# Earlier scores and loads in pieces, scans and high/low parts spread over chunks, sums 128 columns wide, in a fused three-layer block kernel

## The reference

```
first_block:  xn = rmsnorm(x);  q, k, v, xr, gr, ga, gb = split(xn @ w_in)
              ya = banded_attention(q, k, v, rel_bias) @ w_attn_out       (16 heads of 64)
              xc = causal_conv4(xr);  r, i = sigmoid(block matmuls of xc)
              a = exp(-8 r softplus(-lambda));  h = scan(a, sqrt(1-a^2) * i * xc)
              yb = (h * gelu(gr)) @ w_rnn_out
              x += (sigmoid(ga) * ya + sigmoid(gb) * yb) @ w_o
              x += (silu(g) * up) @ w_ffn_out;   x = rmsnorm(x)
second_block: x += gated_deltanet(rmsnorm(x)): q, k, v = silu(conv4(.)), unit-norm q and k,
              decay g and beta from 16 columns, chunks of 128 tokens solved as a triangular
              system, output norm per head, gate silu(z), @ w_out
              x += relu(rmsnorm(x) @ w_up)^2 @ w_down
              x += moba_attention(rmsnorm(x)) @ w_out;  x += mlp;  rmsnorm
```

## Time and profile before

| | |
|---|---|
| median of 3 runs | 1193.99 us (1193.93 to 1196.65) |
| the profiled execution | 1196.81 us |
| its span, first to last instruction | 1195.1 us |
| PE busy | 1144.0 us (96%) |
| DVE busy | 752.3 us (63%) |
| ACT busy | 564.9 us (47%) |
| POOL busy | 219.7 us (18%) |
| mean granted clock of PE | 0.984 |
| read from HBM | 185.29 MB |

### The profile page before, as it was taken

One profiled execution on the slowest core, in us unless ns is written; L12 is line 12 of the kernel. 1 busy time (PEld: TensorE's weight loads), 2 busy tenths in 40 slices (PEclk: granted clock), 3 DMA queues, 4 the chain that ended last, 5 costly groups with the idle time before them and its releaser, 6 DMA issues.

```text
span 1195.1 us, 21847 instructions
## 1 busy us (share of the span) xinstructions
PE 1144.0 (96%) x8900; PEld 1106.9 (93%) x8900; DVE 752.3 (63%) x913; ACT 564.9 (47%) x721; POOL 219.7 (18%) x226
## 2 busy tenths in 40 slices
PE   4999899999999999998999999999989999999997
PEld 4999789999999999998999998889989999888996
DVE  3745975576566543589968567763366757776433
ACT  4546456535454343456635355543344445554331
POOL 4895001502000000246373020000030002000001
PEclk9999999999999999899899999999999999999999
DMA  9654443655555555345420056555535445565541
GB/s 259 225 175 142 141 141 108 199 167 164 176 196 190 177 177 179 103 140 177 137 76 2 9 176 199 181 177 186 188 118 191 163 139 178 179 197 187 175 140 36
DMA packets 154852, 187.34 MB, mean 157 GB/s; under 512 B 6400, under 2 KB 143776, under 8 KB 154784
## 3 DMA queue, kind: packets, MB, share of 16 engines
q1 hardware_dynamic: 149072, 183.51, 47.3%
q10 hardware_dynamic: 5712, 2.86, 0.9%
HBM read 185.29 MB, written 1.07 MB: 156 GB/s over the span
## 4 chain that ended last, share of the span: by engine, by line
PE 86%; DVE 9%; issue 2%; ACT 2%; DMA 1%; POOL 0%; SPq 0%; DVEq 0%; POOLq 0%; ACTq 0%
PE PS L332 20%; PE PS L333 19%; PE PS L334 19%; PE PS L388 10%; PE PS L390 5%; DVE WL L328 2%; DVE XHL L485 1%; PE PS L397 1%; PE PS L396 1%; PE PS L395 1%; ACT WH L319 1%; PE PS L1798 1%; DMA RAW<-in_w_in 1%; PE PS L1784 1%; PE PS L677 1%
## 5 line engine op out<-in xcount | busy, mean ns | idle before, releaser
L328 DVE TENSOR_TENSOR WL<-RAW,WH 128x2048 fp32r<-128x2048 f32 x173 | 409.2, 2366 | 251.8 <-ACT WH L319 251.8
L319 ACT ACTIVATE WH<-RAW 128x2048 fp32r<-128x2048 f32 x173 | 330.0, 1909 | 251.3 <-PE PS L334 203.1
L332 PE MATMUL PS<-XHL,WH 128*128 128x256 f32 x1184 | 346.9, 293 | 27.3 <-DVE WL L328 18.8
L333 PE MATMUL PS<-XHL,WH 128*128 128x256 f32 x1184 | 340.5, 288 | 0.0
L334 PE MATMUL PS<-XHL,WL 128*128 128x256 f32 x1184 | 340.2, 287 | 0.0
L332 PEld LDWEIGHTS PS<-XHL,WH 128*128 128x128 f32 x1184 | 233.2, 197 | 33.1 <-DVE WL L328 18.4
L333 PEld LDWEIGHTS PS<-XHL,WH 128*128 128x128 f32 x1184 | 233.2, 197 | 0.3
L334 PEld LDWEIGHTS PS<-XHL,WL 128*128 128x128 f32 x1184 | 232.7, 197 | 0.0
L332 PE MATMUL PS<-HH,WH 128*128 (+1 forms) x688 | 195.0, 283 | 4.3 <-DVE SG L1581 2.8
L333 PE MATMUL PS<-HL,WH 128*128 (+1 forms) x688 | 194.7, 283 | 0.0
L334 PE MATMUL PS<-HH,WL 128*128 (+1 forms) x688 | 194.7, 283 | 0.0
(11 more groups left out here) (287 smaller groups left out, 1538.3 us busy)
## 6 DMA issues: line engine op xcount, KB each, us to landing
RAW<-in_mlp_w_up SPq DMA_DIRECT2D x32, 1024.0 KB, 5.5
RAW<-in_mlp_w_down SPq DMA_DIRECT2D x32, 1024.0 KB, 4.9
RAW<-in_w_in SPq DMA_DIRECT2D x28, 1024.0 KB, 5.2
RAW<-in_w_ffn_in_pairs SPq DMA_DIRECT2D x22, 1024.0 KB, 5.1
RAW<-in_dn_w_in SPq DMA_DIRECT2D x16, 1024.0 KB, 5.7
RAW<-in_mb_w_in SPq DMA_DIRECT2D x12, 1024.0 KB, 5.2
RAW<-in_w_ffn_out SPq DMA_DIRECT2D x11, 1024.0 KB, 5.0
RAW<-in_w_attn_out SPq DMA_DIRECT2D x4, 1024.0 KB, 5.1
```

The source lines that it names most:

```text
L319: act.activation(WH[:, k], RAW[:, k], ACT.Copy).then_inc(hi_done, 1)
L328: dve.tensor_tensor(WL[:, k], RAW[:, k], WH[:, k].bitcast(F32), ALU.subtract).then_inc(lo_done, 1)
L332: pe.matmul(out, wh, xh, start=start, stop=False, skip_group_check=True)
L333: pe.matmul(out, wh, xl, start=False, stop=False, skip_group_check=True)
```

## The change

- The x parts and chunks 0 and 1 are loaded in quarters: x part, quarter of chunk 0, and so on, then chunk 1's quarters. ACT and DVE split by quarters, PE multiplies chunks 0 and 1 by quarters (`multiply_pieces`), each with a wait of its own.
- The gate weights and the table rows are loaded from SP's queue, between chunks 2 and 3; the decay inputs' rows and the bias from ACT's queue in qk chunk 2. An exp on one column stands first on ACT.
- The first norm: DVE adds the squares instead of POOL, the sums are behind chunk 1 and the rows in the middle of chunk 2 (SUMS_AT 3, ROWS_AT 4). ACT takes the root after the split of chunk 3, DVE the reciprocal after the low half of chunk 3; chunk 0 is read out after that. POOL's preparation of W2, G23 and WBA goes behind the convolution.
- The softplus starts at the head of DVE's list and ends in qk chunk 0; ACT waits for it before the first gate pair (`sp_ready`).
- The roots go from v chunk 1 to v chunk 2. The scans go two blocks each into attention steps 0 to 3.
- The first scores wait for the read-out of the last qk chunk.
- The high and low parts of the gated scan go one by one into the ao chunks, after a wait for the last gab chunk's matmul.
- All sums over partitions with 1, 2 or 16 columns stream 128 columns: ONES whole, W2 and WBA repeated. The results wanted are the first columns. The output norm's columns are in another order.

```diff
@@ names
+        piece_in = [sem(f"piece_in{p}") for p in range(6)]
+        def piece_of(c, p):
+            return (slice(None), c, slice(512 * p, 512 * p + 512))
+        def piece_landed(c, p):
+            return piece_in[3 * c + p] if p < 3 else raw_in[c]
+        def fetch_piece(eng, c, p):
+            dst = RAW[piece_of(c, p)].rearrange("p (k n) -> p k n", k=2)
+            eng.dma_start(dst, source("xr", c)[:, 2 * p:2 * p + 2, :]).then_inc(piece_landed(c, p), 16)
+        def split_hi_piece(act, c, p):
+            act.wait_ge(piece_landed(c, p), 16)
+            act.activation(WH[piece_of(c, p)], RAW[piece_of(c, p)], ACT.Copy).then_inc(s_.hi_piece if p < 3 else hi_done, 1)
+        def multiply_pieces(pe, st):
+            c = st.base
...
+            for p in range(4):
+                if c == 0:
+                    pe.wait_ge(s_.xl_ready, p + 1)
+                if p < 3:
+                    pe.wait_ge(s_.lo_piece, 3 * c + p + 1)
+                else:
+                    pe.wait_ge(lo_done, c + 1)
+                for b in range(2):
+                    part = slice(b * P, b * P + P)
+                    for k in (2 * p, 2 * p + 1):
+                        mm = product(pe, PS[:, c, b * TOK:(b + 1) * TOK], h[:, k, part], l[:, k, part], XH[:, k], XL[:, k],
+                                     k == 0 and b == 0, k == KB - 1)
+            mm.then_inc(mm_done, 1)
-        SUMS_AT = [2, 2, 1, 2, 2, 2]
-        ROWS_AT = [3, 3, 2, 5, 3, 5]
+        SUMS_AT = [3, 2, 1, 2, 2, 2]
+        ROWS_AT = [4, 3, 2, 5, 3, 5]
@@ norm_sums
-                        mm = pe.matmul(PS[:, 4, 2 * c:2 * c + 2], XN[:, j, c * P:(c + 1) * P], W2[:, j],
-                                       start=(j == 0), stop=(j == KB - 1))
+                        mm = pe.matmul(PS[:, 4, 2 * c:2 * c + P].rearrange("p (r e) -> p r e", e=2), XN[:, j, c * P:(c + 1) * P],
+                                       W2[:, j, None, :].to_broadcast([P, P // 2, 2]), start=(j == 0), stop=(j == KB - 1))
...
-                    mm = pe.matmul(PS[:, sums_bank(m), c:c + 1], XN[:, 0, c * P:(c + 1) * P], ONES[:, 0:1], start=True, stop=True)
+                    mm = pe.matmul(PS[:, sums_bank(m), c:c + P], XN[:, 0, c * P:(c + 1) * P], ONES[:], start=True, stop=True)
@@ sync
-            for name, n in SEGMENTS:
-                steps(sp, seg[name], lambda st: fetch(sp, st), head=SLOTS if name == "xr" else 0)
+                fetch_piece(sp, 0, p)
+            for p in range(4):
+                fetch_piece(sp, 1, p)
+            fetch(sp, Step(seg["xr"], 2, None))
+            sp.wait_ge(s_.ext_ready, 1)
+            sp.dma_start(ext_dram, EXT[:]).then_inc(s_.ext_out, 16)
+            sp.wait_ge(s_.wri_zero, 1)
+            sp.wait_ge(s_.pool, 2)
...
+            fetch(sp, Step(seg["xr"], 3, None))
+            for name, n in SEGMENTS[1:]:
+                steps(sp, seg[name], lambda st: fetch(sp, st))
@@ scalar
+            act.wait_ge(s_.const, 1)
+            act.activation(SUM[:, 0:1], EPSC[:], ACT.Exp)
             act.wait_ge(s_.vec_in, 16)
             for p in range(4):
                 norm_high(act, 0, p, squares=False)
+                split_hi_piece(act, 0, p)
+            squares(act, 0, 0)
+            squares(act, 0, 1)
+            act.wait_ge(s_.ey_done, 1)
+            act.activation(SMALL[:, 1, 0:8], SMALL[:, 1, 0:8], ACT.Exp, scale=-1.0).then_inc(s_.sm_ready, 1)
+            for p in range(4):
+                split_hi_piece(act, 1, p)
+            squares(act, 0, 2)
+            squares(act, 0, 3)
...
             for st in (Step(seg["xr"], j, None) for j in range(4)):
                 split_hi(act, st)
-                if st.j == 0:
-                    act.wait_ge(s_.const, 1)
+                if st.j == 1:
                     norm_root(act, 0)
...
             for st in (Step(seg["qk"], j, None) for j in range(8)):
                 split_hi(act, st)
+                if st.j == 2:
+                    late_inputs()
+                if st.j == 0:
+                    act.wait_ge(s_.sp_ready, 1)
                 gate_pair(st.j)
...
-                if st.j == 1:
+                if st.j == 2:
                     root(0)
                     root(1)
...
             for st in (Step(seg["ao"], j, None) for j in range(4)):
+                p = st.j
                 split_hi(act, st)
-            for p in range(4):
+                act.wait_ge(mm_done, seg["ao"].first)
                 act.wait_ge(s_.hs_ready, p + 1)
                 act.activation(XH[:, 2 * p:2 * p + 2], XN[:, 2 * p:2 * p + 2], ACT.Copy).then_inc(s_.yh_done, 1)
@@ vector
             for p in range(4):
                 norm_low(dve, 0, p)
+                split_lo_piece(dve, 0, p)
+            for p in range(4):
+                split_lo_piece(dve, 1, p)
+            dve.wait_ge(s_.sq_done, 4)
+            ch(dve.tensor_tensor(XN[:, 0:4], XN[:, 0:4], XN[:, 4:8], ALU.add))
...
             for st in (Step(seg["xr"], j, None) for j in range(4)):
                 split_lo(dve, st)
                 if st.j == 0:
+                    continue
+                if st.j == 1:
                     norm_scale(dve, ch, 0)
                     dve.wait_ge(s_.wri_zero, 1)
+                    read_out(Step(seg["xr"], 0, None), XR[:, 0:2, 3:TOK + 3])
                 read_out(st, XR[:, 2 * st.j:2 * st.j + 2, 3:TOK + 3])
...
-                if st.j == 3:
-                    scan(0)
...
-                if n == 1:
-                    scan(1)
+                if n < 4:
+                    scan(n)
...
                 split_lo(dve, st)
+                dve.wait_ge(s_.yh_done, j + 1)
+                dve.tensor_tensor(XL[:, blk], XN[:, blk], XH[:, blk].bitcast(F32), ALU.subtract).then_inc(s_.y_done, 1)
                 dve.wait_ge(mm_done, st.count())
@@ tensor
-                if st.j == 1:
+                if st.j < 2:
+                    multiply_pieces(pe, st)
                     pe.wait_ge(s_.const, 2)
-                times_x(0)(st)
+                    norm_point(pe, 0, 2 * st.j + 1)
+                else:
+                    times_x(0)(st)
...
-            c = seg["gr"].first - 1
+            c = seg["v"].first - 1
             pe.wait_ge(freed[c % SLOTS], c // SLOTS + 1)
             pe.wait_ge(s_.gates_done, 16)
             attn_scores(pe, 0)
...
-                            mm = pe.matmul(PS[:, 3, 256 + 16 * c:272 + 16 * c], H[:, k, c * P:(c + 1) * P], WBA[:, k],
+                            mm = pe.matmul(PS[:, 3, 256 + 16 * c:384 + 16 * c].rearrange("p (r e) -> p r e", e=16),
+                                           H[:, k, c * P:(c + 1) * P], WBA[:, k, None, :].to_broadcast([P, KB, 16]),
...
-                        mm = pe.matmul(PS[:, 4 + u, n:n + 1], sq, ONES[:, 0:1], start=True, stop=True)
+                        mm = pe.matmul(PS[:, 4 + u, n:n + P], sq, ONES[:], start=True, stop=True)
...
-                        mm = pe.matmul(PS[:, 4, 8 * c + h:8 * c + h + 1], OSQ[:, h, c * P:(c + 1) * P], ONES[:, 0:1], start=True, stop=True)
+                        mm = pe.matmul(PS[:, 4, 2 * h + c:2 * h + c + P], OSQ[:, h, c * P:(c + 1) * P], ONES[:], start=True, stop=True)
```

More of the change, by code:

```diff
@@ L260, in build @@
           amf_out yf_out ty_out zg_done vn0 vn0_out s_done s_out w_done w_out vn1 vn1_out o_done o_out osq osum osd
-          orows gated uq_zero yy oo low_out""".split()
+          orows gated uq_zero yy oo low_out hi_piece lo_piece sp_ready""".split()
         s = {n: sem(n) for n in names}
@@ L753, in _ @@
                 sp.dma_start(H[:, 2 * p:2 * p + 2], a["x"].rearrange("(j p) t -> p j t", p=P)[:, 2 * p:2 * p + 2]).then_inc(x_in[p], 16)
-            for name, n in SEGMENTS:
-                steps(sp, seg[name], lambda st: fetch(sp, st), head=SLOTS if name == "xr" else 0)
+                fetch_piece(sp, 0, p)
[6 more added lines that the diff above has]
+            sp.wait_ge(s_.pool, 2)
+            for r, w in enumerate(("w_rg_r", "w_rg_i")):
+                for e in range(2):
+                    sp.dma_start(WRI[64 * e:64 * e + 64, r, :, 64 * e:64 * e + 64],
+                                 a[w].rearrange("(j e) d f -> e d j f", e=2)[e]).then_inc(s_.wri_in, 16)
+            fetch(sp, Step(seg["xr"], 3, None))
+            for name, n in SEGMENTS[1:]:
+                steps(sp, seg[name], lambda st: fetch(sp, st))
             for p in range(4):
@@ L809, in _ @@
                         pool.wait_ge(s_.conv_done, j + 1)
+            pool.wait_ge(s_.row_in, 48)
+            fg, g3 = vec_at["final_norm_g"], vec_at["mix_norm_g_2"]
+            pc(pool.memset(W2[:, :, 0:1], 1.0))
+            pc(pool.tensor_tensor(W2[:, :, 1], VEC[:, fg:fg + KB], VEC[:, fg:fg + KB], ALU.mult))
+            pc(pool.tensor_tensor(G23[:], VEC[:, fg:fg + KB], VEC[:, g3:g3 + KB], ALU.mult))
+            pc.wait(pool)
+            pool.tensor_tensor(WBA[:], WBA[:], G23[:, :, None].to_broadcast([P, KB, 16]), ALU.mult).then_inc(s_.prep, 1)
+            pool.wait_ge(s_.prep, 1)
```

(39 more changed lines are left out.)

51 lines of the change are left out of this document (17 added, 34 removed).

## The result

The changed kernel takes 1174.29 us (median, 1173.04 to 1178.35) against 1193.96 (1193.92 to 1196.65) for the kernel before beside it: 0.9836 of it, 95% interval 0.9807 to 0.9864, 19.7 us less. A second series gave 1174.04 against 1194.40: 0.9824 (0.9807 to 0.9842). The forecast was 1171.2, range 1165 to 1180.

What follows compares the result with a forecast made beforehand. TensorE bounds the kernel (86% of the span), so gains come where it waits or runs at half clock: terms of 24.0 less 1.2 charges give 22.8 off 1196.8, less 2.8 for the median: 1171.2 us, range 1165 to 1180.

Steps and rivals of the forecast that it cites:

- the charges of 1.2: Taken off the summed gain: 0.5 for the convolution on POOL and 0.7 for one possible clock fall.
- The charge of 0.7: New short idle stretches before 524 and 679 us may drop the clock: one fall at even odds, 1.7 us.
- Head: Start of the kernel up to the query chunks: PE starts near 7 us, query chunks at 36.3 instead of 45.3, minus 9.0.
- Rival B's first half: Head: pieces move at 227 GB/s (2.7 us); all of B, loads late, head minus 4, 1176 us, 12%.
- Attention: Start of attention: PE's 3.84 us wait and the clock fall after it go, DVE ready 0.7 late; minus 4.8.
- another low half: Start of attention, DVE: second low half before the shift, after one at up to 3.87; minus 4 if POOL slows it too.
- rival C: Start of attention: scores early, but DVE with POOL beside it reaches the shift as late as before; 4.8 back, 1176, 8%.
- Attention output to recurrent output: PE's 1.5 us wait goes as the gated scan's parts move to the attention-output chunks; minus 1.5.
- Norm and decay inputs: Second layer: wide sums keep the clock up, 4.4 for PE, but DVE and ACT then set the pace; minus 2.9.
- Unit norms: Wide sums keep full clock: sums 4.8 to 3.6, chunks 7.7 and 7.2 to 5.75; minus 4.7.
- Output norm: 16 transposes go from 3.40 to 1.75 us at full clock, DVE's products then bind; minus 1.1.
- Rival D: Query chunks: POOL's convolution becomes the bound and the kernel slower; at 11 us a block the time is 1199; 2%.

Runs made afterwards that it cites:

- a_rc: The changed kernel with the first norm's root ahead of chunk 3's split on ACT and the reciprocal ahead of chunk 3's low half on DVE: 1171.84 us.
- a_whole: The changed kernel with chunks 0 and 1 loaded in one load of 1 MB each, splits and products still by quarters: 1175.10 us, ratio 0.9838.
- a_rows: The changed kernel with the three loads for the decay inputs' rows back at the head of ACT's queue, bias still late: 1178.80 us, ratio 0.9862.
- a_shift: The changed kernel with DVE's first attention shift ahead of the second gate chunk's low half, and first scaling ahead of the next low half: 1170.84 us, ratio 0.9798.
- b_sums: The kernel before with only the sums changed, every sum over partitions 128 columns wide: 1187.67 us, ratio 0.9936.
- a_again: The changed kernel run again, unedited, beside the three single parts: 1174.04 us.
- a_root1: The changed kernel with only the roots back in the second v chunk: 1178.04 us.

## Why the prediction came out as it did

**The time.** The forecast was 3.1 below the median. The sum made against the profiled execution (22.8; 23.5 was measured) came close, 1174.0 against 1173.36, in part by luck: attention gave 2.7 less than its term, the head 1.2 and the other parts 1.0 more, and the charges of 1.2 were not used. What put the median off is the frame. I took 2.8 off because the profiled run of before was that much above its median; but the profiled run of after was 0.9 below its own, and the medians differ by only 19.7 and 20.4. What the traces show to differ between runs of the same kernel is when loads land and which idle stretches drop the clock, and a profile shows one draw of that. The places where PE idles, and in how many of the traces the clock fell behind them:

| idle stretch of PE | us | fell |
|---|---|---|
| first scores (kernels with the old wait) | 3.8 | 3 of 3 |
| decay's transposes, 550 | 3.2 | 9 of 14 |
| reciprocal in chunk 2 | 1.9 to 3.7 | 4 of 7 |
| read-out of chunk 0 (a_rc) | 2.1 | 0 of 1 |
| output chunks, 656 (wide sums) | 2.0 | 5 of 10 |
| first transposes of attention | 1.9 to 2.7 | 6 of 8 |
| 30 us into the second block, 508 (wide sums) | 1.7 | 0 of 10 |
| feed-forward's second product | 1.5 | 0 of 14 |

A fall of 3.4 us costs 1.4 to 1.5 at attention and at the output chunks, and nothing at 550, where traces with and without it reach the unit norms' rows equally soon; one of 6.8 there costs 0.9 to 1.1. The charge of 0.7 for one such fall was of the right kind; the wait before the output chunks, at five in ten, is the place.

**Head** (9.0 forecast, 10.2 here, 7.1 to 10.5 over the six traces of this head). The first matmul at 6.9 to 7.4 was right, the wait for the reciprocal too (2.3 against 1.8). The clock rose 4.3 us after the first matmul here (2.9 to 6.2 over the traces) against 7.5 in the sum; but that was not the term that counted. The term is chunk 3's arrival, forecast 23 and measured 21.9, from which the rest follows at the forecast's durations. One step was wrong in kind: I took the early 227 GB/s as the rate at which x lands and the later 341 for the rest, and costed the move of the decay inputs' rows at nothing. Those rows were the cause: putting them back takes the rate to 240 and costs 4.8 us of the median, over half of the head's gain of 8.4. Rival B's first half (pieces are slow) falls with a_whole. The size rule of the Trainium skill that stood behind it, on the page "DMA: Bandwidth & Descriptors", is measured there on loads that GpSimd issues; for SP's loads of 256 KB beside those of 1 MB it doesn't show here. The same page of the Trainium skill has under Specifications a least transfer of 512 bytes for full rate; the packets of a_rows agree with that, and I had not weighed it.

**Attention** (4.8 forecast, 2.1 here). The scores started 0.2 us behind the start of the last V matmul and the old wait went, as forecast; the next late thing was DVE, as forecast, but at 1.9 us instead of 0.7. The step that failed is "another low half" at 2.3 us: POOL's products stretched both low halves, had only one in their reach, and moving the roots by a chunk put them beside two. I had priced that case at 0.8 us; it cost 1.2 of wait, and with it came the fall of the clock that the sum had counted as gone (1.7 forecast, 1.5 measured). It is rival C's mechanism at part strength. a_shift shows it: with one low half out of POOL's way the gain is 4.6. The two POOL products take 2.8 and 4.4 us, and each low half ends about a plain low half's time after a product has ended (107.2 and 111.6). The Trainium skill, "SBUF — State Buffer", section "Who interferes with whom", has it that a DVE instruction with two inputs in SBUF and a GpSimd instruction that reads SBUF lock each other out; low half and root product are such a pair, and the rows agree with blocking rather than sharing.

**Attention output to recurrent output** (1.5): 1.7. **Norm and decay inputs** (2.9): 3.0, and PE's new wait in front of 508 is 1.7 where 1.9 was worked out. **Unit norms** (4.7): 5.6, of which about 1 is the 6.8 us fall behind the 3.2 us wait that the profile of before had; b_sums, with such a fall too, gave 4.7 (the terms written there add to 4.6, not 4.7). **Output norm** (1.1): 0.9. These terms, from counted matmuls at two clock levels, are the ones that held to a few tenths.

**Rival D** (slower) did not happen: 2.8 us of spare where 1.3 was forecast. Its mechanism began to bind once the head was 2 us shorter still.

## What to carry to other kernels

Sum the gain from waits and from counted instructions at the two clock levels, but set it against medians: one profile of before carries its own draw of clock falls, and taking off its excess counts only one of the two draws. Before an instruction is moved on one engine, look at what will then run beside it on its neighbour: two products on POOL stretched two low halves on DVE by 1.6 us each and ate over half of this part's gain. And read the loads of a head for small packets before their sizes: 72 KB, most of it in 64-byte rows, cost 4.8 us; whole chunks in place of quarters cost 1.1, no more than the spread of such medians.

## What the runs showed of the hardware

- Products with 1, 2 or 16 columns, issued back to back, let TensorE's clock fall to its half level although PE shows no idle time; the same sums 128 columns wide cost nearly the same (3.74 us for 32 instructions against 3.63 to 3.68 at the full clock) and never did, in ten traces.
- Idle stretches of 1.9 to 3.2 us drop the clock in some executions of a kernel and not in others; of 1.7 us and less none did in these traces. The half level lasted 3.4 or 6.8 us, apart from the one in which every trace ends.
- After the first matmul the clock rose within 2.9 to 6.2 us; over four traces with the same instructions in the head (after, a_again, a_shift, a_root1) it took 2.9 to 5.5.
- Chunks loaded in 256 KB and in 1 MB moved alike (319 and 317 GB/s over 2 to 8 us); 1509 packets under 512 bytes beside them took the rate to 240.
- A DVE low half of 2.29 us took 3.9 beside a POOL product that reads SBUF.
